# A float32 encoder trunk on one core: feed-forward matmuls in two row halves of TensorE, each for the other token tile

## The reference, cut to what matters

```python
def _swiglu(h, w_in, w_out):                 # w_in 1024 x 5632, w_out 2816 x 1024
    gate, up = jnp.split(h @ w_in, 2, axis=-1)
    return (jax.nn.silu(gate) * up) @ w_out

for l in range(DEPTH):
    x = x + 0.5 * _swiglu(_rmsnorm(x, ffn1_norm[l]), ffn1_w_in[l], ffn1_w_out[l])
    ...  # mixing: gMLP spatial gating for 512 channels, windowed attention for 512
    x = x + 0.5 * _swiglu(_rmsnorm(x, ffn2_norm[l]), ffn2_w_in[l], ffn2_w_out[l])
```

## Time and profile before

| what | us |
|---|---|
| median of three runs | 966.4 (965.08 to 966.95) |
| span of the profiled execution | 966.3 |
| TensorE busy in it | 927.9 (96%) |
| VectorE busy | 515.9 (53%) |
| ScalarE busy | 437.1 (45%) |
| GpSimd busy | 89.2 (9%) |
| share of TensorE in the chain that ended last | 85% |

### The profile page before, as it was taken

The page is one execution under the profiler, slowest core; times in us unless marked ns, Lnnn a source line. Parts: engine busy times, 40 slices in busy tenths (PEclk is TensorE's granted clock), DMA queues, the critical chain, the costliest instruction groups (busy, mean ns, idle before and its releaser), DMA issues.

```text
span 966.3 us, 13023 instructions
## 1 busy us (share of the span) xinstructions
PE 927.9 (96%) x4434; PEld 770.6 (80%) x4434; DVE 515.9 (53%) x574; ACT 437.1 (45%) x515; POOL 89.2 (9%) x133
## 2 busy tenths in 40 slices
PE   8995799999899999999989999999989999999997
PEld 6884588888688888888878888888868888888886
DVE  5641454546575745455357454544666574563542
ACT  7430343436564734343346333524557363442531
POOL 5000200004340000000010000000154000000000
PEclk9997799999999999999999999999999999999999
DMA  8865957354315655746436556473441546555531
GB/s 269 298 129 81 313 188 240 137 184 164 132 42 176 216 177 188 240 135 226 167 111 230 184 195 218 142 247 133 135 171 45 187 171 231 194 166 181 181 125 43
DMA packets 119511, 168.97 MB, mean 175 GB/s; under 512 B 6036, under 2 KB 98256, under 8 KB 119464
## 3 DMA queue, kind: packets, MB, share of 16 engines
q1 hardware_dynamic: 117408, 163.60, 50.1%
q0 software_dynamic: 1696, 4.73, 2.8%
q10 hardware_dynamic: 360, 0.03, 0.0%
HBM read 165.19 MB, written 3.14 MB: 174 GB/s over the span
## 4 chain that ended last, share of the span: by engine, by line
PE 85%; DMA 5%; POOL 4%; issue 3%; DVE 2%; ACT 1%; SPq 0%; ACTq 0%; POOLq 0%; DVEq 0%
PE U L909 17%; PE U L912 17%; PE U L910 16%; PE D L909 5%; PE D L910 5%; PE D L912 5%; PE C L909 5%; PE C L910 5%; PE C L912 5%; DMA raw<-in_ffn_w_in_dram 5%; PE TR L964 2%; POOL rstd L402 2%; PE TR L1043 1%; PE D L1074 1%; POOL mean L401 1%
## 5 line engine op out<-in xcount | busy, mean ns | idle before, releaser
L661 DVE TENSOR_TENSOR w_lo<-raw,w_hi 128x2048 fp32r<-128x2048 f32 (+1 forms) x154 | 346.6, 2270 | 140.4 <-ACT w_hi L474 140.3
L474 ACT ACTIVATE w_hi<-raw 128x2048 fp32r<-128x2048 f32 (+1 forms) x154 | 287.8, 1895 | 71.3 <-DMA raw<-in_ffn_w_in_dram 30.6
L909 PE MATMUL U<-w_hi,xT_hi 128*128 128x512 f32 (+1 forms) x784 | 309.2, 394 | 3.8 <-issue 2.9
L912 PE MATMUL U<-w_hi,xT_lo 128*128 128x512 f32 (+1 forms) x784 | 303.9, 388 | 0.0
L910 PE MATMUL U<-w_lo,xT_hi 128*128 128x512 f32 (+1 forms) x784 | 303.7, 387 | 0.0
L909 PEld LDWEIGHTS U<-w_hi,xT_hi 128*128 128x128 f32 x784 | 148.3, 189 | 33.0 <-issue 3.3
L912 PEld LDWEIGHTS U<-w_hi,xT_lo 128*128 128x128 f32 x784 | 148.4, 189 | 30.7
L910 PEld LDWEIGHTS U<-w_lo,xT_hi 128*128 128x128 f32 x784 | 148.5, 189 | 28.2
L490 ACT ACTIVATE hT_hi<-TR 128x256 fp32r<-128x256 f32 x88 | 29.4, 382 | 246.4 <-PE TR L964 246.4
L673 DVE TENSOR_TENSOR hT_lo<-TR,hT_hi 128x256 fp32r<-128x256 f32 x88 | 33.6, 420 | 172.5 <-ACT hT_hi L490 172.5
L486 ACT ACTIVATE small<-U,inv 128x256 f32<-128x256 f32 x88 | 41.9, 476 | 111.5 <-PE D L912 75.8
(11 more groups left out here) (119 smaller groups left out, 769.8 us busy)
## 6 DMA issues: line engine op xcount, KB each, us to landing
raw<-in_ffn_w_in_dram SPq DMA_DIRECT2D x176, 512.0 KB, 4.7
raw<-in_ffn_w_out_dram SPq DMA_DIRECT2D x88, 512.0 KB, 4.9
raw<-in_w_mix_in_dram SPq DMA_DIRECT2D x28, 512.0 KB, 4.5
raw<-in_w_mix_out_dram SPq DMA_DIRECT2D x16, 512.0 KB, 3.6
bias_rows<-o POOLq DMA_DIRECT2D x1, 2044.0 KB, 46.2
bias<-bias_rows POOLq DMA_DIRECT2D x8, 192.0 KB, 5.8
xs<-in_x_dram SPq DMA_DIRECT2D x2, 512.0 KB, 6.5
out_dram<-xs SPq DMA_DIRECT2D x4, 256.0 KB, 2.0
```

Source lines behind the costliest of these rows:

```text
L474: act.activation(w_hi[:, p % SLOTS, a:], raw[:, p % RAW, a:], ACT.Copy).then_inc(hi_ready, 1)
L661: dve.tensor_tensor(w_lo[:, p % SLOTS, a:], raw[:, p % RAW, a:], w_hi[:, p % SLOTS, a:].bitcast(F32), ALU.subtract).then_inc(lo_ready, 1)
L909: pe.matmul(out_, x_hi, w_hi[:, slot, c], start=start, stop=False)
L912: last = pe.matmul(out_, x_lo, w_hi[:, slot, c], start=False, stop=stop)
```

## The change

In chunks 2 to 10 the 128-row matmuls are replaced by pairs of 64-row matmuls. The two of a pair stand in different row halves of the array, and write to different banks. In a first pass rows 0 to 63 work for tile 0 and rows 64 to 127 for tile 1; in a second pass (swap) the halves change tiles, which completes both sums. Number of columns, products and accumulated terms stay the same. A chunk on TensorE becomes: `enter_pair` u = 0 (first pass), the transposes of h in row halves, `enter_pair` u = 1 (first pass), `leave_pair` of the chunk before (first pass), both `enter_pair` (second pass), `leave_pair` (second pass). A new semaphore `half_rows_in` makes the second pass wait for the end of the first. Chunks 0 and 1, chunk 10's w_out and half of chunk 9's stay as they were. The order on ScalarE and VectorE changes with it, and so does the end of a feed-forward part.

```diff
@@ ScalarE, ffn
+                def chunk(c, j=0):
+                    if c > 2:
+                        silu(L, f, c - 1, 0, j)
+                    silu(L, f, c - 1, 1, j)
                     split(L, pos_in(f, c + 1, 0), j)
-                    if c > 0:
-                        take_hT(L, f, c - 1, 0, j)
-                        take_hT(L, f, c - 1, 1, j)
-                    silu(L, f, c, 0, j)
                     split(L, pos_in(f, c + 1, 1), j)
+                    take_hT(L, f, c - 1, 0, j)
+                    take_hT(L, f, c - 1, 1, j)
                     split(L, pos_out(f, c), j)
...
                 take_hT(L, f, 9, 0)
                 take_hT(L, f, 9, 1)
...
+                    split(L, after[0])
+                silu(L, f, 10, 0)
+                silu(L, f, 10, 1)
+                take_hT(L, f, 10, 0)
+                take_hT(L, f, 10, 1)
+                if after is not None:
                     split(L, after[1])
-                take_hT(L, f, 10, 1)
                 sum_squares(L, 2 * f, 0)
@@ VectorE, ffn
+                def chunk(c, j=0):
+                    if c > 2:
+                        mul(L, f, c - 1, 0, j)
+                    mul(L, f, c - 1, 1, j)
+                    split(L, pos_in(f, c + 1, 0), j)
+                    take_hT(L, f, c - 1, 0, j)
+                    take_hT(L, f, c - 1, 1, j)
                     split(L, pos_in(f, c + 1, 1), j)
                     split(L, pos_out(f, c), j)
...
+                mul(L, f, 10, 0)
+                mul(L, f, 10, 1)
+                take_hT(L, f, 10, 0)
+                take_hT(L, f, 10, 1)
+                if after is not None:
                     split(L, after[1])
-                take_hT(L, f, 10, 1)
                 residual(L, 2 * f, 0)
@@ TensorE
+            HP = P // 2
+            ROWS = (slice(0, HP), slice(HP, P))
+            PRODUCTS = ((0, 0), (0, 1), (1, 0))
...
+                def enter_pair(c, u, swap, j=0):
+
+                    p = pos_in(f, c, u)
+                    if not swap:
+                        if u == 0:
+                            pe.wait_ge(h_done, n_ffn(L, f, c - 1, 1, j))
+                        split_ready(L, p, j)
+                    elif u == 0:
+                        pe.wait_ge(half_rows_in, n_turn(L, f, c, 0, j))
+                    for kk in range(4):
+                        k, cols = 4 * u + kk, slice(kk * 2 * FC, (kk + 1) * 2 * FC)
+                        for lo_x, lo_w in PRODUCTS:
+                            x_, w_ = (xT_lo if lo_x else xT_hi), (w_lo if lo_w else w_hi)
+                            for i in range(2):
+                                t = 1 - i if swap else i
+                                last = pe.matmul(U[t][:, :], x_[ROWS[i], k, t * P:(t + 1) * P], w_[ROWS[i], p % SLOTS, cols],
+                                                 start=not swap and k == 0 and not lo_x and not lo_w,
+                                                 stop=swap and k == KT - 1 and lo_x == 1)
+                    if swap:
+                        last.then_inc(units_used, 1)
+                    elif u == 1:
+                        last.then_inc(half_rows_in, 1)
...
+                def transpose_h_pair():
+
+                    for b in range(4):
+                        kk, t = divmod(b, 2)
+                        for i in range(2):
+                            last = pe.transpose(TR[i][:, b * HP:(b + 1) * HP], h[ROWS[i], t, kk * P:(kk + 1) * P],
+                                                ident[ROWS[i], ROWS[i]])
+                            if b == 3:
+                                last.then_inc(hT_psum, 1)
...
                 def chunk(c, j=0):
-                    enter(c, 0, 0, j)
-                    enter(c, 0, 1, j)
-                    transpose_h(c - 1, 0, j)
-                    transpose_h(c - 1, 1, j)
-                    enter(c, 1, 0, j)
-                    enter(c, 1, 1, j)
-                    leave(c - 1, 0, j)
-                    leave(c - 1, 1, j)
+                    enter_pair(c, 0, False, j)
+                    transpose_h_pair()
+                    enter_pair(c, 1, False, j)
+                    leave_pair(c - 1, (0, 1), False, j)
+                    enter_pair(c, 0, True, j)
+                    enter_pair(c, 1, True, j)
+                    leave_pair(c - 1, (0, 1), True, j).then_inc(units_used, 1)
...
+                enter_pair(10, 0, False)
+                transpose_h_pair()
+                enter_pair(10, 1, False)
+                leave_pair(9, (0,), False)
+                enter_pair(10, 0, True)
+                enter_pair(10, 1, True)
+                leave_pair(9, (0,), True)
+                leave(9, 0, (1,))
                 transpose_h(10, 0)
-                leave(9, 0)
-                leave(10, 0)
                 transpose_h(10, 1)
-                leave(9, 1)
-
-                pe.wait_ge(x_new, n_x_new(L, 2 * f, 0, 1))
+                leave(9, 1, (1,))
+                leave(10, 0).then_inc(acc_ready, 1)
...
```

More of the change, by code:

```diff
@@ L510, in ffn, with by_tile @@
             def ffn(L, f, after):
+                def by_tile(c):
+                    if c > 0:
+                        silu(L, f, c - 1, 1)
+                    split(L, pos_in(f, c + 1, 0))
+                    if c > 0:
+                        take_hT(L, f, c - 1, 0)
+                        take_hT(L, f, c - 1, 1)
+                    silu(L, f, c, 0)
+                    split(L, pos_in(f, c + 1, 1))
+                    split(L, pos_out(f, c))
                 def chunk(c, j=0):
-                    if c > 0:
-                        silu(L, f, c - 1, 1, j)
+                    if c > 2:
+                        silu(L, f, c - 1, 0, j)
+                    silu(L, f, c - 1, 1, j)
                     split(L, pos_in(f, c + 1, 0), j)
-                    if c > 0:
-                        take_hT(L, f, c - 1, 0, j)
-                        take_hT(L, f, c - 1, 1, j)
-                    silu(L, f, c, 0, j)
                     split(L, pos_in(f, c + 1, 1), j)
+                    take_hT(L, f, c - 1, 0, j)
+                    take_hT(L, f, c - 1, 1, j)
                     split(L, pos_out(f, c), j)
[L522 to L525, removed]
+                by_tile(0)
+                by_tile(1)
+                chunk(2)
+                with act.Fori(0, 3) as j:
+                    chunk(3, j)
+                    chunk(4, j)
                 chunk(9)
+                silu(L, f, 9, 0)
                 silu(L, f, 9, 1)
@@ L530, in ffn @@
                 take_hT(L, f, 9, 1)
[L531 to L535, removed]
                 if after is None:
@@ L732, in ffn @@
                 chunk(9)
+                mul(L, f, 9, 0)
                 mul(L, f, 9, 1)
@@ L736, in ffn @@
                 take_hT(L, f, 9, 1)
-                mul(L, f, 10, 0)
-                if after is not None:
-                    split(L, after[0])
-                mul(L, f, 10, 1)
-                take_hT(L, f, 10, 0)
                 if after is None:
@@ new lines, in leave_pair @@
+                def leave_pair(c, kks, swap, j=0):
+                    p = pos_out(f, c)
+                    if swap:
+                        pe.wait_ge(half_rows_in, n_turn(L, f, c + 1, 1, j))
+                    else:
+                        pe.wait_ge(hT_lo_done, n_ffn(L, f, c, 1, j))
+                        split_ready(L, p, j)
+                    for n in range(2):
+                        for kk in kks:
+                            for lo_h, lo_w in PRODUCTS:
+                                h_, w_ = (hT_lo if lo_h else hT_hi), (w_lo if lo_w else w_hi)
+                                for i in range(2):
+                                    t = 1 - i if swap else i
+                                    last = pe.matmul(acc[t][n][:, :], h_[ROWS[i], c % 2, kk, t * P:(t + 1) * P],
+                                                     w_[ROWS[i], p % SLOTS, kk * D + n * 512:kk * D + (n + 1) * 512],
+                                                     start=False, stop=False)
+                    if not swap:
+                        last.then_inc(half_rows_in, 1)
+                    return last
```

123 lines of the change are left out of this document (72 added, 51 removed).

## The result

The changed kernel takes **974.7 us** (median of four runs, 973.68 to 976.43) beside 966.7 for the kernel before (four runs, 965.08 to 968.55): ratio **1.0085, 95% interval 1.0067 to 1.0103**. The profiled execution has a span of 973.4 us, 7.1 more than before, and took 975.04; in every execution with both numbers the time is 1.6 to 1.9 above the span. So the profiled execution of before, with its span of 966.3, took about 968, more than its median, and the spans differ by 7.1 us where the medians differ by 8.1. The forecast was 971.8, the range 954 to 980.

The account below looks back on a forecast made before the run. TensorE, 85% of the chain, was taken to bound the kernel by matmul count, start distance and stops. 966.3 - 6.6 + 0.7 + 7.7 + 3.4 + 0.3 = 971.8 us, range 954 to 980.

Parts of the forecast that it names:

- pairs' surplus: Feed-forward pairs take the scores' 10.8 ns over streaming, 224.1 ns instead of 226.7 each, over 2544 pairs: -6.6 us.
- half transposes: Eight half transposes per chunk, as four pairs, take the time of the four whole ones: 0.
- changes between whole and half rows: Going over to half rows and back costs 0.08 us, twice in each of four parts: +0.7 us.
- table jam: While bias_rows is written, TensorE returns at 108.2 instead of 106.0 with more of the chunk left: +7.7 us.
- ends of parts, f = 0: Six matmuls beside each chain instead of 12 leave stops of 0.7 and about 1.0 us in both parts: +3.4 us.
- ends of parts, f = 1: No split stands there and a loop return or the end follows: 0.15 us each, +0.3 us.
- rival 2: Pairs keep the 13.4 ns surplus in each half, so nothing is gained: 978.4 us; chance 0.12.
- rival 1: Surplus shrinks as alternating halves take turns, a pair costing 218 ns, a gain of 22.1 us: 956.3 us; chance 0.28.
- Rival 3: The table jam costs nothing more because in(5,0) and in(5,1) come earlier in it: 964.1 us; chance 0.08.
- the two covers: In ordinary chunks, second leave_pair (2.7 us) hides the 1.6 us wait for h; hT_lo is ready 1.3 us early: 0.
- Rival 4: Instructions come too slowly: TensorE's doubled loop body stops it at eight inner returns, +46 us: 1018 us; chance 0.05.
- Rival 5: The halves do not overlap over 512 columns, 2544 x 227 ns more: about 1545 us; chance 0.03.

Follow-up runs that it names:

- run 4: Changed kernel, each pair's three products issued for rows 0 to 63, then three for rows 64 to 127: 975.4 us, single run.
- run 6: Changed kernel with each enter_pair matmul cut into two of 256 columns: 995.0 us, single run.
- Run 5: Changed kernel with four 128 x 128 transposes in a paired chunk instead of eight of 64 x 64: 992.1 us, single run.
- run 1: Also no_table_before: kernel before, bias table neither written nor read, no bias or mask in the attention: 943.6 us, ratio 0.9765.
- run 2: Changed kernel with the bias table neither written nor read, no bias or mask in the attention: 942.7 us, ratio 0.9752.
- run 9: Also two_stores_before: kernel before, bias table stored in two parts of four heads, the second 12 units later: 987.2 us, ratio 1.0209.
- run 10: Changed kernel with the bias table stored in two parts of four heads, the second 12 units later: 1004.7 us, ratio 1.0388.
- run 8: Changed kernel, take_hT ahead of both in splits, out(c) split behind silu of chunk c, after[1] split ahead of silu of chunk 10: 965.8 us, ratio 0.9985.
- run 7: Changed kernel with the split of after[1] ahead of silu of chunk 10 on ScalarE and VectorE: 975.1 us, ratio 1.0077.
- run 12: Also new_end: run 8's kernel, new x waited for once behind chunk 9, all 12 leave(10, 1) matmuls beside the chain to xT_lo: 961.4 us, ratio 0.9938.

## Why the prediction was right, and by what

The sign and the mechanism of the loss came out, but that the number did is in part luck: the gain that the sum counted on never came, and gains that it had left out took its place. Worked out span against span, from 966.3 to 973.4:

| term | forecast us | trace us |
|---|---|---|
| pairs' surplus | -6.6 | 0 |
| half transposes | 0 | -5.0 (36 x 0.14) |
| changes between whole and half rows | +0.7 | +1.6 (8 x 0.20) |
| table jam | +7.7 | +8.5 |
| ends of parts, f = 0 | +3.4 | +3.5 |
| ends of parts, f = 1 | +0.3 | +0.9 (0.30 and 0.56) |
| `enter` of chunk 0: a wait less in the first part | not seen | -0.5 |
| start of the first part earlier | not seen | -0.4 |
| outer loop's return shorter | not seen | -1.3 |
| rest | | -0.2 |
| sum | +5.5 | +7.1 |

**The surplus: the step that failed.** "I take that surplus to 512 columns" was the sentence. The scores' 10.8 ns are real, but they don't belong to pairs: paired feed-forward matmuls keep 13.3 ns at 512 and at 256 columns and in either order of issue (runs 4 and 6). This was rival 2's pace, and with the other terms as forecast it gives its 978.4. The chunks of 16.6 us that were to be the sign of faster pairs did come (16.66), but from the transposes. The rule weighed beside rival 1, the span model of the Trainium skill ("TensorE: Matmul & The Clock Gate", "Measured speedup vs the span model"), has one matmul and 4 ns for each further tile: the second half of a pair does start 3 to 4 ns behind the first in most pairs of `enter_pair` (16 to 17 in most of the others), but the next pair comes 226.7 ns after, so the rule fits one pair and not a row of them.

**The transposes: a term set to 0 without a row.** "Four pairs in the time of four" was wrong by 0.14 us a chunk: eight half transposes start in 0.22 us, four whole ones in 0.36. Run 5 shows that half rows save 0.34 more, which I had not even asked about: whole transposes would need two changes in each chunk.

**The table jam: right, in its mechanism too, and 0.8 too small.** Forecast: store at 55.5 and its end at 102.1, in(5,1) at 105.2, TensorE back at 108.2. Trace: 54.7, 101.1, 105.9, 109.0. Chunk 5 is 7.4 us late, though TensorE was 1.0 us early at the first transposes (28.68 against 29.64), gained 0.4 with three shorter transposes and lost 0.2 on the way into halves: the jam itself is 7.4 + 1.0 + 0.4 - 0.2 = 8.5 us from unrounded starts. Within the 7.4 both parts were off: the return is 3.0 later and not 2.2, and the work behind it takes 12.7 us instead of 8.4, 4.4 more and not 5.5, because the half clock lasted 3.7 us there and not the 6.0 of before. The result and runs 1, 2, 9 and 10 (-0.9, +8.1 and +17.5 us with no, one and two jams) carry the cause, run 8 the step: it is the order on ScalarE and VectorE. Rival 3 (the jam costs nothing more) is out.

**Ends of parts.** Stops of 0.7 and 1.0 us forecast, 0.56 and 1.19 found. The reason I gave for the first, VectorE's low part of after[1] ahead of the residual, holds for two thirds: with that moved away (run 7) 0.37 us of it went. The other 0.18 is the residual sum beside only six matmuls; no run put more there. The second stop has the cause that was forecast: with twelve matmuls beside the chain instead of six (run 12) it is gone. For f = 1 the same residual wait costs 0.3 and 0.6 us where I had 0.15.

**Missed in the diff.** `enter` of chunk 0 now waits for xT_lo of its own half of the contraction only (`n_tran(L, 2 * f, t, u)` where the last argument was 1). In the first part of the kernel before, tile 1 waited for the second half; its matmul starts 0.70 us behind the one before it, and in the kernel after no such distance is left, 0.5 us less:

```profile
18.61 0.50 PE L909 MATMUL U<-w_hi,xT_hi 128*128 128x512 f32 x1 [0.32 <-DVE xT_lo L702]
```

Two other gains look like the same thing and aren't. The part's first matmul starts 0.4 us earlier, at 11.31 instead of 11.67; but it waits for w_lo of the first weights, and in the profiles of the kernels with the change it starts anywhere from 11.16 to 11.97. And the outer loop's return fell from a distance of 3.28 us (496.93 to 500.20, most of it in the earlier trace rows) to 2.00. In the kernel before xT_lo was complete before the last matmul of the part had even started:

```profile
495.55 1.29 DVE L702 TENSOR_TENSOR xT_lo<-sc,xT_hi 128x512 fp32r<-128x512 f32 x2
496.93 0.39 PE L912 MATMUL D<-w_hi,hT_lo 128*128 128x512 f32 x1
```

The same return took 2.42 us in two_stores_before and 2.25 in no_table_before, 1.73 to 2.14 in the kernels with the changed end of a part, and 0.61 in new_end, where xT_lo is complete early as well. So about 0.9 of the 1.3 us belongs to the one profiled execution of before, and what holds the return where xT_lo doesn't is not shown. The waits of the kernel after (us in total, times, longest) have the return and the two stops before KV in one line:

```profile
PE U L950 <- DVE xT_lo L729: 3.6, 3, 1.6
```

**The other rivals.** No wait for h or hT_lo in an ordinary chunk: the two covers held. Rival 4 is out, no inner return stops (in the list of waits TensorE has none in a loop of chunks besides the jam), and run 6 goes on at 30 ns an instruction. Rival 5 is out, the halves do overlap. Rival 1 is out.

## What to carry to other kernels

Price a new kind of instruction by its distance from start to start in its own use, and give no term 0 because its work stays the same: the transposes were the gain and the pairs were not. Where a long transfer holds up loads, an in-order engine's queue decides what the stall costs: put what others wait for ahead of the splits that wait for loads, and ask of each split which load it stands behind. And at the end of a stage count the matmuls between the last one that the chain needs and the wait for the chain: the same work in another order gave some 4 us back, 1.3 of it at the outer loop's return.

## What the runs showed of the hardware

- A pair of 64-row float32r matmuls, each with its own weights, keeps the full matmul's surplus over streaming: 13.3 ns at 512 columns and at 256, in either order (226.7 and 120.0 ns a pair). The scores' 10.8 ns stay unexplained.
- Going over from whole rows to halves or back cost 0.17 to 0.20 us.
- Eight transposes of 64 x 64 in row halves start in 0.22 us, the four of 128 x 128 that they replace in 0.36.
- The store of the table went by packets of 0.9 us, at most 8 at a time with eight heads and 4 with four, and half of it took as long as the whole, 46 us.
- The granted clock fell to 0.50 (1.2 GHz) in the long stop, from 82.0 us on in the kernel after (TensorE had stopped at 79.4), and was back at 112.7, 3.7 us behind TensorE's return. Short stretches at 0.50 stand in one execution and not in another: behind the outer loop's return before and in the second layer's mixing part after (some 1.6 us each, so that they cancel in the table of terms), and near the start in new_end, where eight matmuls start 0.43 us apart and cost 1.6 us of the profiled span.
